# First projection from scaled x with its shift added afterwards, scale blocks loaded first, masks loaded late

## The reference

```python
mod = jax.nn.silu(c) @ w_ada[l] + b_ada[l]            # 6 x 1024 columns per token kind
shift1, scale1, gate1, shift2, scale2, gate2 = jnp.split(mod, N_MOD, axis=-1)
h = _rmsnorm(x, norm1_g) * (1.0 + scale1) + shift1
z = jnp.einsum('bld,dc->blc', h, w_in)                # q, v, zf, zb, og, u, gz
...
u = u[..., :CONV_DIM] * jax.nn.sigmoid(u[..., CONV_DIM:])   # then a depthwise convolution
```

## Time and profile before

| | us |
|---|---|
| median of 3 runs | 880.71 |
| lowest, highest | 879.78, 884.81 |
| the profiled execution, its own time | 879.61 |
| its span, first to last instruction | 877.5 |
| PE busy | 814.0 (93%) |
| DVE, ACT, POOL busy | 389.9, 223.0, 69.3 |
| mean granted TensorE clock | 0.976 of full speed |
| moved by DMA | 284.71 MB, 324 GB/s over the span |

### The profile page before, as it was taken

The page is one execution under the profiler, slowest core; times in us unless marked ns, Lnnn a source line. Parts: engine busy times, 40 slices in busy tenths (PEclk is TensorE's granted clock), DMA queues, the critical chain, the costliest instruction groups (busy, mean ns, idle before and its releaser), DMA issues.

```text
span 877.5 us, 13010 instructions
## 1 busy us (share of the span) xinstructions
PE 814.0 (93%) x5306; PEld 558.9 (64%) x5306; DVE 389.9 (44%) x781; ACT 223.0 (25%) x344; POOL 69.3 (8%) x53
## 2 busy tenths in 40 slices
PE   3799999999999989999999999699999999799964
PEld 2488989899999979974554545264554735354222
DVE  1236899779989656664233322122221111122104
ACT  3124343434435144321121211011111111011002
POOL 1000465800000010100000000000000000000000
PEclk9799999999999999999999999899999999899997
DMA  8979888234243539978899999999999999999993
GB/s 313 387 278 354 289 287 297 88 119 169 97 153 137 161 121 350 392 276 328 359 417 416 418 414 420 414 417 419 416 417 410 417 415 419 416 418 419 416 407 120
DMA packets 80917, 284.71 MB, mean 324 GB/s; under 512 B 5208, under 2 KB 11736, under 8 KB 64216
## 3 DMA queue, kind: packets, MB, share of 16 engines
q1 hardware_dynamic: 80360, 282.06, 82.5%
q10 hardware_dynamic: 496, 1.79, 0.5%
HBM read 280.67 MB, written 3.16 MB: 323 GB/s over the span
## 4 chain that ended last, share of the span: by engine, by line
PE 72%; DMA 10%; SPq 10%; DVE 3%; POOL 2%; issue 2%; ACT 0%; DVEq 0%; POOLq 0%
PE bank L2008 15%; PE bank L2064 8%; SPq L602 8%; PE bank L1617 6%; PE bank L1625 5%; PE bank L1619 5%; DMA chunk<-in_w_expert_down 5%; PE bank L1893 4%; PE bank L1916 4%; PE bank L1605 3%; PE bank L1680 3%; DMA chunk<-in_w_expert_gate_up 3%; DMA ring<-in_w_ada 2%; PE bank L1640 2%; PE bank L1573 2%; PE bank L1644 2%
## 5 line engine op out<-in xcount | busy, mean ns | idle before, releaser
L2008 PE MATMUL bank<-chunk,xg 128*64 128x512 f32 (+2 forms) x1024 | 203.1, 627 | 20.9 <-DMA chunk<-in_w_expert_gate_up 19.3
L2008 PEld LDWEIGHTS bank<-chunk,xg 128*64 128x64 f32 (+2 forms) x1024 | 63.1, 131 | 153.8 <-issue 137.8
L2064 PE MATMUL bank<-chunk,act_t 128*64 128x512 f32 (+2 forms) x512 | 101.0, 612 | 4.0 <-DMA chunk<-in_w_expert_down 3.8
L1431 DVE SCALAR_TENSOR_TENSOR act_r<-bank,w_slot,sil 128x256 f32<-128x256 f32 x26 | 12.6, 484 | 183.0 <-ACT sil L939 183.0
L1443 DVE TENSOR_TENSOR y_lo<-bank,y_hi 128x512 fp32r<-128x512 f32 x52 | 36.0, 692 | 74.1 <-ACT y_hi L952 74.1
L2064 PEld LDWEIGHTS bank<-chunk,act_t 128*64 128x64 f32 (+2 forms) x512 | 31.2, 128 | 52.4 <-issue 51.6
L939 ACT ACTIVATE sil<-bank 128x256 f32<-128x256 f32 x26 | 10.0, 384 | 212.9 <-PE bank L2008 212.9
L1045 DVE TENSOR_TENSOR ring_lo<-ring,ring_hi 128x1024 fp32r<-128x1024 f32 x44 | 52.7, 1220 | 19.4 <-ACT ring_hi L752 19.2
L656 POOL TENSOR_TENSOR small<-small 128x4 f32<-128x4 f32 (+2 forms) x9 | 9.2, 1024 | 653.5 <-DVE small L1513 489.2
L952 ACT ACTIVATE y_hi<-bank 128x512 fp32r<-128x512 f32 x52 | 31.0, 597 | 102.5 <-PE bank L2064 102.5
L1076 DVE SCALAR_TENSOR_TENSOR conv<-upad,dw,conv 128x256 f32<-128x256 f32 x120 | 54.6, 525 | 0.0
(11 more groups left out here) (309 smaller groups left out, 1293.9 us busy)
## 6 DMA issues: line engine op xcount, KB each, us to landing
chunk<-in_w_expert_gate_up SPq DMA_DIRECT2D x128, 1024.0 KB, 21.0
chunk<-in_w_expert_down SPq DMA_DIRECT2D x64, 1024.0 KB, 22.8
ring<-in_w_in SPq DMA_DIRECT2D x16, 2048.0 KB, 10.1
ring<-in_w_ada SPq DMA_DIRECT2D x12, 2048.0 KB, 13.5
ring<-in_w_proj_hgrn SPq DMA_DIRECT2D x2, 2048.0 KB, 8.2
ring<-in_w_out SPq DMA_DIRECT2D x2, 2048.0 KB, 13.8
ring<-in_w_proj_conv SPq DMA_DIRECT2D x1, 2048.0 KB, 8.4
chunk<-in_w_shared_gate_up SPq DMA_DIRECT2D x2, 1024.0 KB, 23.9
```

What stands on the lines that cost most here:

```text
L2008: ins = mm(bank[2 + b][row:row + width, :], xg[:, k, c:c + width], w[:, k % 4, :], start=(k == 0), stop=(k == KD - 1))
L2064: ins = mm(out[row:row + width, :], act_t[:, c, row:row + width], w[:, c, h * 512:(h + 1) * 512], start=(c == 0), stop=(c == 1))
```

## The change

- The first transfer on SP is the first scale block (ada2), then both halves of x, then ada3, u1, ada0, ada1, and only then the masks and the router bias, then ada4, u2. All small vectors, and `consts` without its masks, go out on ACT's queue.
- The table `ADA` renumbers the partial sums: 2, 3, 0, 1, 4 and so on. After ada2 and ada3 DVE has scale1 and makes `gain1`. The normalised, transposed x is multiplied with it into `x_gained`, two banks by DVE and two by ACT (scale as a per-partition operand).
- u1 is projected from `x_gained`. The partial sums and sums of ada0 and ada1 (shift1) run inside u1's projection. Behind it PE multiplies u1's weights with the shift (32 matmuls with 128 x 128 weights and 2 columns), DVE copies the 8 results to `u1_bias` and adds them in u's gating.
- `h1_hi` is now x_gained plus shift, 16 ACT operations of 128 x 128; `h1_lo` is (x_gained plus shift) minus `h1_hi`, 16 DVE operations. `h1_lo` lies where `h1_rest` was and serves all blocks; `h1_rest` is gone.

```diff
         h1_hi = at("h1_hi", 168, [P, KD, T], F32R)
-        h1_lo = at("h1_lo", 160, [P, KD, T], F32R)
+        h1_lo = at("h1_lo", 104, [P, KD, T], F32R)
+        x_gained = at("x_gained", 152, [P, KD, T])
...
+        ADA = (2, 3, 0, 1, 4, 5, 6, 7, 8, 9, 10, 11)
...
+        for name in ("ada2", "ada3", "u1", "ada0", "ada1", "ada4", "u2", "q0", "ada5", "zf0", "ada6", "zb0", "ada7", "q1", "ada8", "zf1", "ada9", "zb1",
+                     "ada10", "v0", "ada11", "v1", "og0", "og1", "ga0", "ga1", "gb0", "gb1"):
...
+        for name, n in zip(("u2", "q0", "ada5", "zf0", "ada6", "zb0", "ada7", "q1", "ada8", "zf1", "ada9", "zb1", "ada10", "ada11"),
+                           (3, 0, 2, 1, 3, 0, 2, 1, 3, 0, 2, 1, 3, 3)):
+            place[name] = n
...
-            sp.dma_start(x_tok[:, 0, :], A["x_prompt"][0]).then_inc(s_x, 16)
-            for x, dst in loads_small[0::2]:
-                sp.dma_start(dst, x).then_inc(s_rows, 16)
-            sp.dma_start(x_tok[:, 1, :], A["x_sample"][0]).then_inc(s_x, 16)
...
+            load_block("ada2")
+            for s, x in enumerate((A["x_prompt"], A["x_sample"])):
+                sp.dma_start(x_tok[:, s, :], x[0]).then_inc(s_x, 16)
+            for name, _ in blocks[1:-2]:
                 load_block(name)
+                if name == "ada1":
+                    sp.dma_start(consts[:, C_MASK:C_TRI], A["consts"][:, C_MASK:C_TRI]).then_inc(s_wr, 16)
+                    sp.dma_start(b_router[:, :], A["router_bias"].broadcast_to([P, NE])).then_inc(s_wr, 16)
...
-            act.dma_start(consts[:, :], A["consts"]).then_inc(s_cst, 16)
-            for x, dst in loads_small[1::2]:
+            for x, dst in loads_small:
                 act.dma_start(dst, x).then_inc(s_rows, 16)
+            for c in (slice(C_ID, C_MASK), slice(C_TRI, C_ALL)):
+                act.dma_start(consts[:, c], A["consts"][:, c]).then_inc(s_cst, 16)
...
+            evacuate_u1(0)
+            copy_partial(2)
+            copy_partial(3)
+            act.wait_ge(mod_done, 4)
+            for k in range(KD):
+                for s in range(NS):
+                    ins = nc.scalar.activation(h1_hi[:, k, s * P:(s + 1) * P], x_gained[:, k, s * P:(s + 1) * P], ACT.Identity, bias=mod_v[:, M_SH1 + k, s:s + 1])
+                ins.then_inc(h1_hi_done, 1)
+            split_hi(0, (0, 1))
+            evacuate_u1(1)
+            split_hi(0, (2, 3))
...
-            modulation(0, 16, 4)
-            gains(gain1, M_SC1, R_G1)
-            for j in range(4):
+            modulation(8, 16, 2, 2)
...
+                        ins = V.tensor_scalar(x_gained[:, k, s * P:(s + 1) * P], src, gain1[:, 2 * k + s:2 * k + s + 1], None, ALU.mult)
                 ins.then_inc(dve_evac, 1)
+            modulation(0, 8, 4, 4)
+            evacuated(dve, "h3")
+            for k in range(KD):
+                dve.wait_ge(h1_hi_done, k + 1)
+                for s in range(NS):
+                    c = slice(s * P, (s + 1) * P)
+                    ins = V.scalar_tensor_tensor(h1_lo[:, k, c], x_gained[:, k, c], mod_v[:, M_SH1 + k, s:s + 1], h1_hi[:, k, c].bitcast(F32), ALU.add, ALU.subtract)
+                ins.then_inc(h1_lo_done, 1)
...
+                        ins = V.scalar_tensor_tensor(uu, uu, u1_bias[:, b:b + 1], sg[:, c, s], ALU.add, ALU.mult)
...
+            def ada_within_u1(q, k):
+
+                if (q, k) == (2, 0):
+                    ada_partial(2)
+                if (q, k) == (3, 0):
+                    ada_sum(2)
+                    ada_partial(3)
+                if (q, k) == (3, 4):
+                    ada_sum(3)
+
+            project("u1", x_gained, before_k=lambda k: evacuated(pe, f"h{k // 2}"), after_k=ada_within_u1)
+            pe.wait_ge(mod_done, 4)
+            for c in range(4):
+                for k in range(KD):
+                    ins = mm(bank[6][:, 2 * c:2 * c + 2], tile_of("u1")[:, k, c * P:(c + 1) * P], mod_v[:, M_SH1 + k, :], start=(k == 0), stop=(k == KD - 1))
+            ins.then_inc(u1_bias_ready, 1)
+            ada_partial(4)
```

More of the change, by code:

```diff
@@ L722, in copy_partial @@
                 nc.scalar.activation(tmp[:, j % 2, :], bank[4 + j % 2][:, :], ACT.Copy).then_inc(part_copied, 1)
+            act.wait_ge(s_x, 32)
+            for s in range(NS):
+                own.mark(nc.scalar.activation(xn[:, s, :], x_tok[:, s, :], ACT.Square, accum_out=ssq[:, s:s + 1]))
+            copy_partial(0)
             for j in range(4):
@@ L727, in _ @@
                                      ACT.Copy).then_inc(act_evac, 1)
-            own.wait()
-            for j in range(4):
-                copy_partial(j)
+            copy_partial(1)
             act.wait_ge(s_init, 3)
-            for j in range(4):
-                evacuated(act, f"h{j}")
-                nc.scalar.activation(h1_hi[:, 2 * j:2 * j + 2, :], h_t[:, 2 * j:2 * j + 2, :], ACT.Copy).then_inc(h1_hi_done, 1)
+            act.wait_ge(gain1_done, 2)
+            for j in (1, 3):
+                filled(act, f"h{j}")
+                for kk in range(2):
+                    for s in range(NS):
+                        k = 2 * j + kk
+                        src = fill_bank(f"h{j}")[:, kk * T + s * P:kk * T + (s + 1) * P]
+                        ins = nc.scalar.activation(x_gained[:, k, s * P:(s + 1) * P], src, ACT.Copy, scale=gain1[:, 2 * k + s:2 * k + s + 1])
+                ins.then_inc(act_evac, 1)
             def split_hi(n, quarters):
@@ L752, in split_hi, with evacuate_u1 @@
                     nc.scalar.activation(part_hi(n, q), tile_of(split[n])[:, :, q * P:(q + 1) * P], ACT.Copy).then_inc(w_hi_done, 1)
-            for j in range(2):
+            def evacuate_u1(j):
                 filled(act, "u1", j)
@@ L1007, in _, with modulation @@
                 V.tensor_scalar(xn[:, s, :], x_tok[:, s, :], rms[:, s:s + 1], None, ALU.mult).then_inc(xn_done, 1)
-            def modulation(j0, j1, ready):
+            def modulation(j0, j1, ready, n):
                 dve.wait_ge(mod_ready, ready)
@@ L1047, in _ @@
             split_lo(0, range(4))
+            dve.wait_ge(u1_bias_ready, 1)
+            own.step(V.tensor_copy(u1_bias, bank[6][:, 0:8]))
             for j in range(2):
@@ L1053, in _ @@
                 for c in range(2):
[L1054 to L1055 removed]
+                    for s in range(NS):
+                        uu = upad[:, 2 * j + c, s, PAD:PAD + P]
+                        b = 2 * (2 * j + c) + s
+                        ins = V.scalar_tensor_tensor(uu, uu, u1_bias[:, b:b + 1], sg[:, c, s], ALU.add, ALU.mult)
                 ins.then_inc(u_gated, 1)
[L1057 to L1059 removed]
             dve.wait_ge(u_gated, 2)
@@ L1124, in og_gate @@
                     ins.then_inc(dve_evac, 1)
-            modulation(16, 48, 12)
+            modulation(16, 48, 12, 6)
             gains(gain2, M_SC2, R_G2)
@@ L1559, in to_channels @@
                 return ins
-            for j in range(4):
-                to_channels((f"xt{j}", 0), x_tok, j).then_inc(proj_ready, 1)
             def ada_partial(j):
-                arrived(f"ada{j}")
+                arrived(f"ada{ADA[j]}")
                 if j >= 2:
                     pe.wait_ge(part_copied, j - 1)
-                w = tile_of(f"ada{j}")
+                w = tile_of(f"ada{ADA[j]}")
                 for k in range(KD):
@@ L1657, in quarter @@
                 pe.wait_ge(w_lo_done, 4 * n + 2 * half + 2)
-                pe.wait_ge(h1_rest_done, 4)
+                pe.wait_ge(h1_lo_done, KD)
                 hi, lo = column_half_hi(n, half), column_half_lo(n, half)
-                for x, w in ((h1_hi, hi), (h1_hi, lo), (h1_rest, hi)):
+                for x, w in ((h1_hi, hi), (h1_hi, lo), (h1_lo, hi)):
                     for k in range(KD):
                         ins = mm(out, x[:, k, s * P:(s + 1) * P], w[:, k], start=(half == 0 and x is h1_hi and w is hi and k == 0),
-                                 stop=(half == 1 and x is h1_rest and k == KD - 1))
+                                 stop=(half == 1 and x is h1_lo and k == KD - 1))
                 if q == 1:
```

127 lines of the change are left out of this document (54 added, 73 removed).

## The result

| | forecast | measured |
|---|---|---|
| median, us | 879.3 (874.8 to 885.2) | 889.63 (888.54 to 891.54, 7 runs) |
| against before | | ratio 1.0097, interval 1.0073 to 1.0121; before 880.71 (879.02 to 884.81, 7 runs) |
| the profiled execution, own time and span | 878.2 | 889.63 and 887.6 (before 879.61 and 877.5) |
| first instruction of PE | 10.2 | 16.72 (before 10.18) |
| first matmul of u1 | 27.1 | 32.08 (before 41.06) |

The account below looks back on a forecast made before the run. The start of u2 was taken to decide the span. PE's chain puts u1 at 27.1 us, 28.9 us more plus 1.0 for the clock puts u2 at 57.0, 1.4 sooner: 878.2 own time, median 879.3 us (874.8 to 885.2).

Parts of the forecast that it names:

- allowance for the clock ahead of u1: 1.0 us added for low clock in PE's chain before u1, a quarter of the 3.9 us more seen at low clock.
- u1's release by x_gained: Sign of being right: u1's first matmul near 27 to 29 us, waiting for x_gained and not for its weights.
- the cover of h1_hi and h1_lo: Between u1's last sum and u2: 8.8 us of ACT and DVE work hidden in 9.9 us, only under the shift products.
- the wait of q0 behind u2's last sum: The wait at 72.47 us for w_lo stays, since ACT splits q0 only after u2's last sum.
- The late one: Late bound of PE's wait for small vectors and consts: 12.5 us; early bound 6.0, taken 10.2.
- one queue now carries 13 of them beside a 2 MB block: Argument against rival 1's sooner first wait, about the small transfers on ACT's queue.
- 32 of them are 6.3 us: Shift products behind u1, priced from the sum's 4 matmuls in 0.79 us; 12.1 us as upper bound.
- rival 2: Clock falls in the shift products: 12.1 us there, ada4 3.12; 7.1 us slower than forecast, 886.4 us; chance 0.13.
- stretches as full of weight loads later keep clock 1.00: Argument against rival 2's falling clock in the shift products, beside PE being full before them.
- the 2.9 us that it adds if transposes cool the clock too: Rival 2's extra cost if the transposes ahead of u1 also lower the clock: 2.9 us more.
- Rival 1: PE's first wait ends sooner, at 7.5 instead of 10.2 us, clock up throughout; 3.7 us together, 875.6 us; chance 0.24.
- Rival 3: Chain ahead of u1 at low clock through transposes (2.9 us), or x late at 15.5 us (1.6); 882.2 or 880.9; chance 0.20.

Follow-up runs that it names:

- a4_few_products: Changed kernel with 4 instead of 32 shift products, so its output differs and experts get more work; 926.79 us, u2's first matmul at 58.55 us.
- a5_blocks_wait: Changed kernel with SP issuing its first scale block only after all small vectors and consts have landed; 887.41 us, PE's first instruction at 7.71 us.
- a3_small_split: Changed kernel with half the small vectors on SP ahead of the first block, the rest on ACT behind consts; 885.09 us.
- f1_padded: e3_x_first with the two shift columns padded to 32 and four groups of output rows in turn; 874.57 us, ratio 0.9924 to the kernel before.
- c1_spread: Changed kernel with its 32 shift products spread: 16 behind u1, 8 behind each of u2's first two quarters; 887.93 us.
- b32_products: Kernel before the change plus 32 unused 2-column products behind u1, weights from h_t outside the ring; 892.06 us.
- b16_products: Kernel before the change plus 16 unused 2-column products behind u1, weights from h_t; 885.38 us.
- e3_x_first: Changed kernel with shift columns as weights (8 wide matmuls), small vectors split over SP and ACT, u1's inner sums earlier, x before the first block; 878.92 us.

## Why the prediction was wrong, step by step

| step | forecast | after | difference, us |
|---|---|---|---|
| PE's first instruction | 10.2 | 16.72 | +6.5 |
| from there to the first partial sum, and its length | 1.6, 3.46 | 1.62, 3.64 | +0.2 |
| transposes of x and of xn | 5.2 | 2.02 and 1.80 | -1.4 |
| sums, copy, modulation, scaling, second partial sum | 6.6 | 6.3 | -0.3 |
| u1's own matmuls | 15.45 | 16.2 | +0.8 |
| two partial sums and two sums in u1 | 5.28 | 5.28 | 0 |
| shift products | 6.3 | 10.82 | +4.5 |
| ada4 | 1.85 | 3.57 | +1.7 |
| allowance for the clock ahead of u1 | 1.0 | not needed | -1.0 |
| first matmul of u2 | 57.0 | 67.99 | +11.0 |

**What bounds the kernel, right.** The premise held that u2's start decides: +9.6 there against before, +10.5 at the first expert, +10.1 in the span. So did u1's release by x_gained, the cover of h1_hi and h1_lo (7.4 us of work in a4_few_products, 16.2 us from the last sum to u2 in the changed kernel), the masks, for which nothing waits in the chain up to u2, and the wait of q0 behind u2's last sum, which now ends with ACT at 84.45 us (with DVE's w_lo at 73.84 before, +10.6).

**The first step that failed: "The late one is the last issue's start, 5.6, plus the 6.9 us that the router bias took", 12.5 us as the upper bound.** The last transfer took 10.7 us from its issue to PE, beyond both ends. The 6.9 us were measured where all small transfers had been issued ahead of the first block. The change itself takes that away, and puts a stream of some 400 GB/s next to them. That was seen ("one queue now carries 13 of them beside a 2 MB block") and set against a gain only; it should have raised the upper bound. a5_blocks_wait shows the size, 9 us, and a3_small_split what it was worth in the whole, 4.5 us. In the sum the step is the 10.2 us of the first instruction, which measured 16.72.

**The second step that failed: "32 of them are 6.3 us", with rival 2 at 0.13.** The mechanism of rival 2 happened: the clock fell in the shift products. It cost 4.5 and 1.7 us, 6.2 together, against the 7.1 of its working. The argument against it ("stretches as full of weight loads later keep clock 1.00") took the weight loads as the likeness. The stretch of 70 to 72 us above is as full of them, 2.00 us of 2, and its clock is 1.00. What differs between the two is what is moved for each load, 256 columns there and 2 in the products. No run varied that alone, so what it is in the products that lets the clock fall stays open; that it falls, and what it costs, is shown. The row that spoke for it, the clock of 0.50 at 36.8 to 41 us with sums and transposes, was the nearest one. Even rival 2's 886.4 lies below the result, since no rival held the late first wait. With the 2.9 us that it adds if transposes cool the clock too it comes to 889.3, close to the result by luck: those 2.9 us did not come, and the first wait stands in their place. In the own time of the profiled execution the steps do add up: 878.2 and the 11.0 us at u2 are 889.2, for 889.63 measured.

**Rival 1** (a sooner first wait) went the other way in the change. Its early start came with a3_small_split, at 6.94 us, but not its time. **Rival 3** did not happen in the changed kernel: the transposes ran in 2.02 and 1.80 us and the partial sum behind them in 1.90, at clock 1.00. The 1.6 us that it names for a late x do not follow from its rows (15.5 and 6.4 make 21.9, 3.2 behind the 18.7 of the sum, 1.9 without the table load of 1.28 us); nothing came of it, since PE itself started after x had landed. By the Trainium skill's sentence on transposes (TensorE: Matmul & The Clock Gate, Part 4: PE-mode transpose) 2.9 us more were to come, and this trace shows none of them.

Slow transposes of xn were seen once, in the profiled execution of f1_padded, with 3.52 us where the ten other traces of the changed order have 1.80 to 1.97. Together with the slow pieces around them they cost 4.5 us. Whether the transposes had a part in the low clock these runs do not tell.

## What to carry to other kernels

A latency read from a trace holds for the company in which it was measured. When a change puts large transfers ahead of or beside the small ones that the first instruction waits for, do not bound that wait by its old latency (16.72 us beside the blocks here, 7.71 alone), and keep small vectors ahead of the first block.

A busy PE did not mean a full clock: a run of 32 products of 2 columns was paid twice here, in itself and in the clock of what followed. Turned round with padded weights and several groups of output rows the same product cost 1.9 us instead of 10.8. And when a consumer is spread out or moved, look at which buffer it releases (8 us for ada5 in c1_spread).

## What the runs showed that was not expected

- Thirteen small transfers, under 0.4 MB in all, let PE start at 7.71 us alone and at 16.72 us beside the blocks and x.
- PE busy without a gap was granted half the clock: within the 2-column products in the changed kernel, b32_products and c1_spread, and right behind 3.47 us of them in b16_products, with weights in the ring and outside it.
- PE's first long piece ran at half its usual pace although its granted clock reads 1.00: the first partial sum of the changed kernel took 3.64 us (18.34 to 21.98), the next 1.90. In e3_x_first, where the transposes of x come first, those took 3.50 us and the first partial sum 1.97. A clock of 1.00 at the start of a trace did not mean full pace; why is open.
- Passes of 512 columns with 2-column weights into the same two output rows took 0.43 us each; with 32-column weights into four groups of rows in turn, 0.12 (1.92 us for 16).
- With one and the same order of PE's work ahead of u1, the granted clock at 16 to 20 us was 1.00 in one execution (e3_x_first) and 0.50 in another (f1_padded), worth 4.5 us.
